# A 257th column of y that holds epsilon, and a second group whose B filter and C.B product come earlier

## What is computed

```python
def mamba2_bidir_branch(z, xbc, dt_raw, conv_w, conv_b, a_log, dt_bias, d_skip, norm_g, w_out):
    xbc = jax.nn.silu(depthwise_conv_centred(xbc, conv_w, conv_b))       # 5 taps
    xs, Bm, Cm = jnp.split(xbc, [D_INNER, D_INNER + N_GROUPS * D_STATE], axis=-1)
    ...
    y_f = ssd_chunked(xs, dt_f, A[0], Bm, Cm)
    y_b = flip(ssd_chunked(flip(xs), flip(dt_b), A[1], flip(Bm), flip(Cm)))
    y = y_f + y_b + xs.astype(jnp.float32) * d_skip[:, None]
    y = y.reshape(b, s, D_INNER) * jax.nn.silu(z.astype(jnp.float32))
    yg = y.reshape(b, s, N_GROUPS, D_INNER // N_GROUPS)
    yg = yg * lax.rsqrt(jnp.mean(jnp.square(yg), axis=-1, keepdims=True) + RMS_EPS)
    y = (yg.reshape(b, s, D_INNER) * norm_g).astype(z.dtype)
    return y @ w_out
```

## Time and profile before

| what | value |
|---|---|
| median of 3 runs | 2376.46 us (2375.77 to 2377.34) |
| the profiled execution | 2375.51 us |
| its span, first to last instruction | 2373.9 us, granted TensorE clock 1.000 |
| busy: PE / DVE / ACT / POOL | 99% / 62% / 57% / 20% |
| DMA | 402.79 MB, mean 170 GB/s |

### The profile page before, as it was taken

One profiled execution on the slowest core, in us unless ns is written; L12 is line 12 of the kernel. 1 busy time (PEld: TensorE's weight loads), 2 busy tenths in 40 slices (PEclk: granted clock), 3 DMA queues, 4 the chain that ended last, 5 costly groups with the idle time before them and its releaser, 6 DMA issues.

```text
span 2373.9 us, 34460 instructions
## 1 busy us (share of the span) xinstructions
PE 2338.9 (99%) x11448; PEld 1936.3 (82%) x11448; DVE 1463.9 (62%) x2570; ACT 1356.1 (57%) x2239; POOL 476.6 (20%) x589
## 2 busy tenths in 40 slices
PE   8999999999999999999999999999999999999999
PEld 6878888887777888888788787888878778888886
DVE  4899898989545211113758999989895461111147
ACT  5756657366564554344757566664755655544446
POOL 2322222222111111111113122221321111111110
PEclk9999999999999999999999999999999999999999
DMA  7676575857888788888775856747578877889985
GB/s 206 142 168 152 124 176 119 185 125 161 179 186 202 169 192 193 191 208 190 158 159 121 185 125 160 176 110 169 133 173 182 185 188 179 193 192 197 211 189 137
DMA packets 112252, 402.79 MB, mean 170 GB/s; under 512 B 12401, under 2 KB 12401, under 8 KB 112113
## 3 DMA queue, kind: packets, MB, share of 16 engines
q0 software_dynamic: 54144, 195.06, 48.0%
q1 hardware_dynamic: 55728, 200.56, 26.2%
q10 hardware_dynamic: 2240, 5.42, 0.6%
HBM read 398.89 MB, written 2.10 MB: 169 GB/s over the span
## 4 chain that ended last, share of the span: by engine, by line
PE 84%; ACT 7%; DVE 6%; issue 2%; DMA 1%; POOL 0%; SPq 0%; POOLq 0%; ACTq 0%; DVEq 0%
PE bank L882 23%; PE bank L884 23%; PE bank L883 23%; PE bank L924 3%; PE bank L925 3%; PE bank L927 3%; ACT decay L517 2%; PE bank L1001 1%; PE bank L1007 1%; PE bank L1221 1%; ACT w_lo L466 1%; DVE tmp_m L1403 1%; ACT y_hi L536 1%; DMA w_raw<-w_stream 1%; PE bank L1019 1%
## 5 line engine op out<-in xcount | busy, mean ns | idle before, releaser
L882 PE MATMUL bank<-x_hi,w_hi 128*128 128x512 f32 x1728 | 686.0, 397 | 1.7 <-DMA w_lo<-w_stream 1.7
L884 PE MATMUL bank<-x_hi,w_lo 128*128 128x512 f32 x1728 | 673.4, 390 | 0.0
L883 PE MATMUL bank<-x_lo,w_hi 128*128 128x512 f32 x1728 | 672.7, 389 | 0.0
L362 POOL DMA_DIRECT2D w_lo<-w_stream x376 | 327.3, 870 | 1646.8 <-ACT w_lo L466 1592.3
L465 ACT ACTIVATE w_hi<-w_raw 128x1024 fp32r<-128x1024 f32 (+1 forms) x378 | 400.3, 1059 | 272.4 <-PE bank L884 250.4
L466 ACT ACTIVATE w_lo<-w_raw 128x1024 fp32r<-128x1024 f32 (+1 forms) x378 | 397.6, 1052 | 0.0
L882 PEld LDWEIGHTS bank<-x_hi,w_hi 128*128 128x128 f32 x1728 | 324.6, 188 | 70.5 <-issue 2.9
L884 PEld LDWEIGHTS bank<-x_hi,w_lo 128*128 128x128 f32 x1728 | 324.4, 188 | 68.8
L883 PEld LDWEIGHTS bank<-x_lo,w_hi 128*128 128x128 f32 x1728 | 324.7, 188 | 67.9 <-issue 3.4
L1316 DVE SCALAR_TENSOR_TENSOR z_a<-glu_out,params,z_a 128x497 f32<-128x497 f32 (+14 forms) x480 | 320.7, 743 | 0.0
L1793 DVE TENSOR_TENSOR glu_out<-bank,sigmoids 128x512 f32<-128x512 f32 x44 | 30.4, 692 | 404.1 <-PE bank L884 404.1
(11 more groups left out here) (256 smaller groups left out, 3571.5 us busy)
## 6 DMA issues: line engine op xcount, KB each, us to landing
w_raw<-w_stream SPq DMA_DIRECT2D x362, 512.0 KB, 5.1
w_lo<-w_stream POOLq DMA_DIRECT2D x360, 512.0 KB, 7.6
w_raw<-w_stream SPq DMA_DIRECT2D x16, 384.0 KB, 3.8
w_lo<-w_stream POOLq DMA_DIRECT2D x16, 384.0 KB, 5.8
z_b<-x_in SPq DMA_DIRECT2D x4, 512.0 KB, 6.3
out<-z_b SPq DMA_DIRECT2D x4, 512.0 KB, 6.2
ple_p<-p_in ACTq DMA_DIRECT2D x2, 512.0 KB, 6.5
w_ple_in<-w_ple ACTq DMA_DIRECT2D x2, 512.0 KB, 11.7
```

The lines of the kernel that those rows point to most:

```text
L362: gp.dma_start(wlo[:, s, 0:n], w_stream[cyc, s, :, 0:n].bitcast(F32R), accum_op=ALU.add).then_inc(lo_done[s], 16)
L882: pe.matmul(dst, wh, mh, start=first, stop=False)
L883: pe.matmul(dst, wh, ml, start=False, stop=False)
L884: return pe.matmul(dst, wl, mh, start=False, stop=last)
```

## The change

y gets 16 more columns per chunk, of which column 256 holds a constant, sqrt(256 epsilon), set by DVE once per layer. ACT's square reads 257 columns, so that its sum is the mean square plus epsilon, and POOL's addition and its semaphore step go. The filter of the second group's B tile is taken out of the joint filter of B and C: it stands alone ahead of the first group's `entering`, and the filter of C stays where both were. On PE `c_dot_b` of the second group comes first, then `b_transpose`, then exponent 1; `c_dot_b` waits for `yl_done` itself; the mask waits for the third count of `tr_done` in the second group, the B tokens for the fourth.

```diff
@@
-        mse = sb("mean_squares_eps", [P, CH])
...
-        sb("fill_to_line", [P, 16])
+        sb("fill_to_line", [P, 16 + CH])
...
-            y = sb("y_tok", [P, CH, GW], F32, r)
+            y = sb("y_tok", [P, CH, GW + 16], F32, r)
...
-            junk = sb("squares", [P, GW], F32, r)
+            junk = sb("squares", [P, GW + 1], F32, r)
@@ group_rms, POOL
-                gp.tensor_scalar(mse[:, c], ms[:, c], RMS_EPS, None, ALU.add).then_inc(rms_done, 1)
-                gp.wait_ge(rms_done, seen(4 * G + 2 * part + 1))
-                gp.tensor_tensor(rst[:, c], mse[:, c], neghalf[:, c], ALU.pow).then_inc(rms_done, 1)
+                gp.tensor_tensor(rst[:, c], ms[:, c], neghalf[:, c], ALU.pow).then_inc(rms_done, 1)
@@ b_tokens, ACT
-            def b_tokens(G):
-                act.wait_ge(tr_done, seen(4 * G + 3))
+            def b_tokens(G, late=0):
+
+                act.wait_ge(tr_done, seen(4 * G + 3 + late))
@@ square, ACT
+                if G % GROUPS == 0:
+                    act.wait_ge(eps_ready, G // GROUPS + 1)
...
-                act.activation(junk[:, :], y[:, c, :], ACT.Square, scale=GW ** -0.5,
+                act.activation(junk[:, :], y[:, c, 0:GW + 1], ACT.Square, scale=GW ** -0.5,
@@ pair, ACT
-                b_tokens(G1)
+                b_tokens(G1, 1)
@@ c_dot_b, PE
                 pe.wait_ge(tok_evac, seen(3 * G + 2))
+                pe.wait_ge(yl_done, seen(2 * G))
@@ pair, PE
+                c_dot_b(G1)
+                b_transpose(G1)
                 exponent(G1, 1)
-                b_transpose(G1)
-                c_dot_b(G1)
@@ new, DVE
+            def conv_one(g, G, i, cyc, s, ns=None):
+
+                dve.wait_ge(evac[s], seen(cyc + 1))
+                dve.wait_ge(tr_done, seen(4 * G))
+                if i == 3:
+                    dve.wait_ge(yo_done, seen(CH * G))
+                w, b = group_par(g, i * TAPS, TAPS), group_par(g, 4 * TAPS + i)
+                out, x = feat[:, i, :], cin[:, i, :]
+                mid = TAPS // 2
+                for n, k in list(enumerate([mid] + [k for k in range(TAPS) if k != mid]))[slice(*(ns or (0, TAPS)))]:
+                    o = k - mid
+                    a, e = max(0, -o), T - max(0, o)
+                    if n == 0:
+                        step(dve.tensor_scalar(out, x, w[:, k:k + 1], b, ALU.mult, ALU.add))
+                        continue
+                    dve.wait_ge(dve_order, issued())
+                    q = dve.scalar_tensor_tensor(out=out[:, a:e], in0=x[:, a + o:e + o], scalar=w[:, k:k + 1],
+                                                 in1=out[:, a:e], op0=ALU.mult, op1=ALU.add)
...
@@ mask_cb, DVE
-            def mask_cb(G):
-                dve.wait_ge(tr_done, seen(4 * G + 4))
+            def mask_cb(g, G):
+
+                dve.wait_ge(tr_done, seen(4 * G + 4 - g % 2))
@@ normalise_y, DVE
-                    dve.wait_ge(rms_done, seen(4 * G + 2 * part + 2))
+                    dve.wait_ge(rms_done, seen(2 * G + part + 1))
@@ start of a layer, DVE, after the dt bias
+                dve.memset(y[:, :, GW:GW + 1], (RMS_EPS * GW) ** 0.5).then_inc(eps_ready, 1)
@@ order of a pair, DVE
                     mix(g0, G0, 1)
+                    conv_one(g1, G1, 2, c0 + 2, 0)
                     entering(g0, G0)
...
                     normalise_y(G0, (0,))
-                    conv(g1, G1, 2, [(c0 + 2, 0), (c0 + 2, 1)], (0, 1))
+                    conv_one(g1, G1, 3, c0 + 2, 1, (0, 1))
                     normalise_y(G0, (1,))
-                    conv(g1, G1, 2, [(c0 + 2, 0), (c0 + 2, 1)], (1, TAPS))
+                    conv_one(g1, G1, 3, c0 + 2, 1, (1, TAPS))
                     rest_of_y(0, g0, G0)
```

More of the change, by code:

```diff
@@ L259, in build @@
         ss_done = sem("ss_done")
+        eps_ready = sem("eps_ready")
         rms_done = sem("rms_done")
@@ L1322, in taps @@
                     between(n)
+            def conv_one(g, G, i, cyc, s, ns=None):
[15 more added lines that the diff above has]
+                                                 in1=out[:, a:e], op0=ALU.mult, op1=ALU.add)
+                    if n == TAPS - 1:
+                        q.then_inc(conv_done, 1)
+                    else:
+                        step(q)
             def conv(g, G, i, tiles, ns=None):
@@ L1413, in within @@
                     dve.wait_ge(xd_ready, seen(G + 1))
-                dve.tensor_tensor(y[:, c, :], y[:, c, :], bank[6 + c % 2][:, 0:GW], ALU.add).then_inc(yd_read, 1)
+                dve.tensor_tensor(y[:, c, 0:GW], y[:, c, 0:GW], bank[6 + c % 2][:, 0:GW], ALU.add).then_inc(yd_read, 1)
             def outputs(g, G, c):
@@ L1434, in outputs @@
                 dve.wait_ge(yd_read, seen(CH * G + c + 1))
-                step(dve.tensor_tensor(y[:, c, :], y[:, c, :], ty[:, 0, :], ALU.add))
+                step(dve.tensor_tensor(y[:, c, 0:GW], y[:, c, 0:GW], ty[:, 0, :], ALU.add))
                 dve.wait_ge(dve_order, issued())
-                dve.tensor_tensor(y[:, c, :], y[:, c, :], ztok[:, c // 2, (c % 2) * GW:(c % 2 + 1) * GW],
+                dve.tensor_tensor(y[:, c, 0:GW], y[:, c, 0:GW], ztok[:, c // 2, (c % 2) * GW:(c % 2 + 1) * GW],
                                   ALU.mult).then_inc(yg_ready, 1)
@@ L1441, in normalise_y @@
                 for part in parts:
-                    dve.wait_ge(rms_done, seen(4 * G + 2 * part + 2))
+                    dve.wait_ge(rms_done, seen(2 * G + part + 1))
                     for c in ((0, 1, 2), (3,))[part]:
-                        r = dve.tensor_scalar(y[:, c, :], y[:, c, :], rst[:, c:c + 1], None, ALU.mult)
+                        r = dve.tensor_scalar(y[:, c, 0:GW], y[:, c, 0:GW], rst[:, c:c + 1], None, ALU.mult)
                         if c < CH - 2:
@@ L1670, in _ @@
                         long_filter(j - 1, (CONV_A - LATER, CONV_A))
-                    mask_cb(G0)
+                    mask_cb(g0, G0)
                     mix(g0, G0, 0)
@@ L1690, in _ @@
                     weighted_xs(g1, G1, 1)
-                    mask_cb(G1)
+                    mask_cb(g1, G1)
                     mix(g1, G1, 0)
```

## The result

The changed kernel takes 2382.57 us (median of 10 runs, 2379.71 to 2384.29), the kernel before 2376.86 us (median of 10, 2375.74 to 2380.47): ratio 1.0021, 95% interval 1.0012 to 1.0029. It is slower by 5.7 us; inside the range forecast, above the 2378.2 that was named as likeliest, and where the first rival put it (2381.7 to 2384.6). The line of 0.2% that the forecast drew between same and slower lies within the interval. The profiled execution took 2382.94 us, its span is 2381.3.

A forecast was written before the change was run, and what follows sets the result against it. PE, busy 99% of the span, was taken as the bound; per pair +0.43 us stall, -0.27 and +0.06 at the end gave +0.22, over eight pairs +1.8 us: forecast 2378.2 us, range 2372.5 to 2385.

The forecast's parts named there:

- the first rival: Both GpSimd selects run ahead of entering and hold VectorE: stall 0.86 to 1.22 us, 2381.7 to 2384.6 us, chance 0.31.
- a stall at the entering product: PE waits at chunk 0's second matmul for entering states delayed by the selects: 0.43 us per pair.
- a small gain at the pair's end: Before the transposes of y: 0.27 us won by epsilon, 0.06 lost to ACT's later copy, per pair.
- the slower rival: The same as the first rival: selects hold VectorE in entering, +5.2 to +8.1 us, chance 0.31.
- Step 1, epsilon: Dropping POOL's addition lets scaling of y start right behind the GLU product: 0.27 us gained per pair.
- Step 2, the filter: B filter ahead of entering leaves 0.38 us to spare, but selects fall into entering: PE stalls 0.43 us.
- the price of the selects: Time two GpSimd selects cost VectorE in entering: taken as 0.81 us, with ends of none and 1.60.
- unhindered stall of zero: Without the selects, entering ends at 229.47, 0.38 us ahead of PE's need, so PE doesn't stall.
- the price of turns: Selects meeting a back-to-back VectorE stream alternate with it: 0.40 us per select, 0.81 for two.
- the row I had put above it: Trace row of selects within a multiply-add stream, 0.40 us each, preferred to the skill's full blocking with stall 0.88.
- Step 3, C.B first: DVE's mask starts 0.90 us earlier, but decays bind and ACT's copy comes later: net -0.06 us per pair.
- The faster rival: The earlier mask moves each pair's end by 1.17 us: -9.4 us, 2367.1 us, chance 0.13.

The follow-up runs named there:

- experiment 4: Changed kernel, with GpSimd waiting for the entering states before the two selects of the second group's first exponent: 2376.10 against 2377.63 us for the kernel before, 0.9995.
- experiment 5: Changed kernel, with GpSimd issuing the two selects ahead of the weight DMA instead of behind it: 2378.46 against 2377.51 us for the kernel before, 1.0007.
- Experiment 6: Kernel before, with only the C.B product put first on PE, then transposes, then exponent 1: 2378.44 against 2377.51 us, 1.0006.
- experiment 10: Changed kernel with the B filter back as before and ACT's third copy of states moved into the decays of chunk 2: 2371.69 against 2377.33 us before, 0.9977.
- 2: Changed kernel with the B filter back in the joint filter, epsilon and C.B first kept: 2375.35 against 2377.63 us for the kernel before, 0.9992.

## Why the prediction was right, and where it was not

**The sign and the range** hold, and by the mechanism named: a stall at the entering product that outweighs a small gain at the pair's end. The size doesn't: +1.8 us was named as likeliest, +5.7 measured. The range held it because it was drawn, 12.5 us wide, to take in the slower rival, to which I had given 0.31.

**Step 1, epsilon.** As worked out. In the second pair scaling starts 0.60 behind the GLU product, PE's wait is 1.25 instead of 1.52 us, 0.27. Alone it gives -1.0 us in the medians, -2.2 had been the sum; the interval holds both.

**Step 2, the filter.** Its own arithmetic holds: 3.57 us were worked out, 3.60 measured. The term that failed is the price of the selects. "By that it is nearest to the stream, and I take 0.81": measured 1.49, near the end that I had kept for the slower rival (1.24 to 1.60). The unhindered stall of zero is confirmed by experiment 4, the price of turns (0.91 against 0.81) by experiment 5, where the order on POOL is another. The premise that failed is that a VectorE stream without a gap takes turns with the selects: DVE had no gap and was held nevertheless. What decides is open (experiment 5). With 1.49 in place of 0.81 the prediction's own sum gives a stall of 229.47 + 1.49 - 229.85 = 1.11 us, beside 1.03 measured. The whole with what was measured: six stalls, 6.8 us in all, and eight times -0.27, 6.8 - 2.2 = +4.6 us, against +5.7 in the medians. No run pins the 1.1 us between them; the waits on `w_lo` differ by more than that from profile to profile. That two of eight pairs would escape was not foreseen; with 1.08 in all eight it would have been +6.4.

The first group's later work cost nothing, as written: L1001 has no wait in either list.

**Who blocks whom.** The traces show one 256-wide instruction held over both selects, 1.49 us. The Trainium skill, "SBUF — State Buffer", Who interferes with whom, has the loser blocked for whole instructions; worked out before as a stall of 0.88, beside 1.03 measured. For this stall the rule was the better guide than the row I had put above it; for experiment 5, where the two took turns, it wasn't. Its sentence "Issue order, not op shape, decides who blocks" is not borne out by the starts in the trace: the instruction that stood was issued at 229.21 (the first of its row at 228.88, the second 0.33 later), the first select at 229.25. In the first pair it was the other way round: the select started at 88.26 and waited, the last L1401, 0.33 behind the start of its row at 88.06, ran in its usual time.

**Step 3, C.B first.** The outcome is as worked out: the mask 0.9 us earlier, L1433 0.1. Experiment 6 gives it no gain. On the way POOL's selects took 0.50 us of the 0.9, where 0.8 to 1.2 had been priced, and the wait for the eighth decay the rest. That the reordered matmuls cost PE nothing holds too: from the first of them to the second dense matmul behind them it is 2.03 us before and after.

```profile
254.37 0.28 PE L970 MATMUL bank<-seg_rhs,tri_early_half 128*128 128x256 f32 x1
...
256.40 0.39 PE L883 MATMUL bank<-x_lo,w_hi 128*128 128x512 f32 x1
```

```profile
256.94 1.05 PE L957 MATMUL bank<-xs_b_c 128*128 128x128 f32 x8
...
258.97 0.40 PE L884 MATMUL bank<-x_lo,w_hi 128*128 128x512 f32 x1
```

**The faster rival** (the earlier mask gets through) was rightly small, but my reason was incomplete. I named the decay as what is late next; behind it stood a second ACT instruction, the third copy of states, that would have eaten the same gain. Rows 8 had it, with 0.2 us idle, and I used it only to carry 0.06 us.

## What to carry to other kernels

When an instruction run is moved ahead of a deadline, look not only at its length but at what another engine will then be issuing during the run that has the deadline; a reserve of 0.4 us is worth nothing if two selects of another queue now fall into it. A gain that ends in a wait on engine X should be followed through all of X's later hand-overs before it is booked: here the mask's 0.9 us died first at POOL's selects and a decay and, once that was filled, at a copy of states. Moving that copy up by four activations was worth 3.4 us (experiment 10 against 2), more than any of the three parts of the change.

## What the runs showed of the hardware

- Two GpSimd selects met VectorE's stream of 256-wide instructions with two inputs (entering) in three ways. 0.55 us behind a DMA issue of GpSimd's and 1.05 us into the stream they cost VectorE 1.49 us, one instruction held through both. Ahead of the DMA issue and 0.04 us into the stream the two engines took turns, 0.91 us (experiment 5). 0.55 us behind a DMA issue again, but at the end of the stream, in the first pair of a layer, they cost VectorE nothing, and took 2.33 us themselves instead of 1.26. What decides among the three isn't settled; a DMA issue just ahead doesn't by itself, nor does the order in which the trace shows the instructions to start.
- The DMA issue alone, in the middle of the same stream, cost VectorE nothing (experiment 4).
